# Meta keys' share of the attention outputs: one stacked fp32r product in place of one float32 product

## The chip, the cores and the metric

The kernel runs on one core of one Trainium2 chip. The metric is the device time of one execution in microseconds (us), the median of several runs. TensorE (PE) does the matrix products, with loads of the stationary operand (PEld) as records of their own; VectorE is DVE, ScalarE is ACT, GpSimd is POOL, and SyncE (SP) issues the DMAs.

## The reference, cut to what matters

Two layers; each has an input projection of 9,216 columns, eight HGRN2 heads, eight differential-attention heads and an output projection. There are 512 tokens and 16 meta tokens in front of them, 528 rows in all. The part that the change touches is this:

```
s = einsum('bqhcd,bkhcd->bhcqk', qblk, kh) * scale     # 528 keys, the first 16 are the meta tokens
p = softmax(s, axis=-1)
p_diff = p[:, :, 0] - lam * p[:, :, 1]
o      = einsum('bhqk,bkhv->bqhv', p_diff, vh)          # 528 keys contracted: 4 x 128 + 16
```

## The kernel before

Everything is kept transposed, features in partitions and tokens in columns. A projection unit is a tile of 128 output columns, accumulated over 8 pieces; each piece is three fp32r products (high weight by high input, high by low, low by high), in two halves of 264 tokens or, where the meta rows are not wanted, once over 512 (`piece`, L1797). The heads of a layer come one after another; each is cut into steps, and after each step `feed` puts some pieces of the next head's units, of the output projection's too, into TensorE's program. All orders are written out by hand, in five programs (SP, POOL, ACT, DVE, PE) that meet in semaphores.

An attention head (heads 8 to 15 of a layer) works in chunks of 128 queries, two steps to a chunk, one for each of the two softmax components. Layer 0 has five chunks (the fifth is the 16 meta queries), layer 1 has four. For chunk i and component comp, step s = 2i + comp does, engine by engine:

- PE: waits for the exponential of step s-1 (`exp_done`), then computes the scores into `pair` (L2041, L2043). In odd steps from 3 on it turns the difference of the softmaxes of chunk j = i-1: four 128-column transposes (L2072) and one of the 16 meta columns (L2073), into `main` and `meta`. In even steps from 4 on it computes the output of chunk j = i-2 (L2058, L2060), then come the fed pieces.
- DVE: the row maximum (`neg_max`, L1652) of each step; in even steps from 2 on, L1671, L1673 and L1681 make the difference `qk_dec` of chunk j = i-1 and raise `p_ready`. Between them stand the halves' cut of the weights (`w_lo`, L1265), the scaled copies out of PSUM (L1330), the rotary turn (L1424, L1426, L1437, L1442) of the next head's queries and keys, and the low parts of the stacked queries and keys (L1449).
- ACT: the exponential of each step (L1078, with a second record for its sum); `copy_turned`, which brings the turned probabilities to SBUF (L1061 the four blocks, L1064 the meta block; raises `pt_ready`); the output rows (L1091, L1098); the high cut of the weights (`w_hi`, L848); and `stack_high`, the high parts of the next head's stacked queries and keys (L1112), which for the keys waits for DVE's L1442.

ACT's program of a layer-1 head has the keys' `stack_high` in step 8 and `copy_turned` of chunk 3 in step 9, so the second stands behind the first.

The output of one chunk:

```
for kk in range(4):
    pe.matmul(meta[:, 0:P], cols[:, kk, :], v_main(kk), start=(kk == 0), stop=False)
pe.matmul(meta[:, 0:P], cols[:, 4, :], v_meta[:, :], start=False, stop=True).then_inc(pv_done, 1)
```

All five are float32. The last contracts 128 rows, of which 16 are meta keys and the rest zero. `v_meta` is made by `turn_v` (a transpose of 16 columns, L1898) and ACT's `copy_v`.

Of the kernel before, what the change touches and what calls it, by code (L numbers as in the profile page):

```python
# [31 lines left out]
P = 128  # L32
DEPTH = 2
D_MODEL = 1024
N_META = 16
# [3 lines left out]
HG_HEADS = 8  # L39
AT_HEADS = 8  # L40
# [14 lines left out]
LEVELS = 8  # L55
META_LEVELS = 5
HG_TILES = ("zf", "zb", "q", "v", "g")
AT_TILES = ("aq", "ak", "av", "ag")
# [296 lines left out]
def encoder_trunk(nc, x_t, w_units, norm_g, lb_logits, hg_gain, lambdas, at_gain, final_g,  # L355
# [9 lines left out]
    with ctx:  # L365
# [56 lines left out]
        lam_in = state_f[:, :, :].rearrange("p a (b d) -> p a b d", b=2)  # L422
        lam_prod = state_b[:, 0:DEPTH, :].rearrange("p a (b d) -> p (a b) d", b=2)
        score = sb("score", [P, N_CHUNKS, P])
        blend = sb("blend", [P, N_CHUNKS, HALF_CHUNK])
# [49 lines left out]
        v_written = sem("v_written")  # L475
        v_landed = sem("v_landed")
        v_turned = sem("v_turned")
        v_ready = sem("v_ready")
# [214 lines left out]
        def facing_totals(m, first):  # L693
# [7 lines left out]
                           ap=[at.ap[0], [stride, 2], [2, n_pairs], [0, m]])  # L701

        def v_main(j):

            return v_rows[:, :, j, :]
# [89 lines left out]
        def _(pool):  # L795
# [8 lines left out]
            pool.memset(k_low[:, :, :].bitcast(f32), 0.0).then_inc(pads_set, 1)  # L804
            pool.memset(parity[:, :, :], 0.0).then_inc(pads_set, 1)

            def invert_rms(n):

                pool.wait_ge(sq_ready, n + 1)
                if n > 0:  # L810
                    pool.wait_ge(o_scaled, n)
                pool.tensor_scalar(o_inv[:, :], o_sums[:, :], P * NORM_EPS, None, ALU.add)\
                    .then_inc(pool_step, 1)
                pool.wait_ge(pool_step, n + 1)
                pool.tensor_tensor(o_inv[:, :], o_inv[:, :], minus_half[:, :], ALU.pow)\
                    .then_inc(o_inv_ready, 1)

            def cut_mixed(n):
# [6 lines left out]
            for l in range(DEPTH):  # L825
                for c in range(HEADS):
                    n = l * HEADS + c
                    if c > 0:
                        cut_mixed(n - 1)
                    invert_rms(n)  # L830
                cut_mixed(l * HEADS + HEADS - 1)
# [3 lines left out]
        def _(act):  # L835
# [121 lines left out]
            def copy_v(n):  # L957
                act.wait_ge(v_turned, n + 1)
                act.activation(v_meta[0:N_META, :], meta[0:N_META, 0:P], ACT.Copy).then_inc(v_ready, 1)

# [96 lines left out]
            def copy_turned(a, j, chunks_before):  # L1057
# [5 lines left out]
                                    ACT.Copy))  # L1063
                act.activation(cols[0:N_META, 4, 0:rows], meta[0:N_META, 0:rows], ACT.Copy)\  # L1064
                    .then_inc(pt_ready, 1)

# [57 lines left out]
            act.wait_ge(ones_set, 4)  # L1124
            act.wait_ge(pads_set, 6)
            load_root_table()
# [73 lines left out]
        def _(dve):  # L1200
# [455 lines left out]
            def attend(l, c, s):  # L1656
# [10 lines left out]
                if comp == 0 and 1 <= i < 1 + chunks:  # L1667
# [8 lines left out]
                    if j >= 2:  # L1676
# [4 lines left out]
                    dve.scalar_tensor_tensor(qk_dec[r, j % 2, 0, :], e1, row_inv[r, j % 2, 1:2], e0,  # L1681
                                             ALU.mult, ALU.add).then_inc(p_ready, 1)

            dve.wait_ge(gain_in, 16)
# [85 lines left out]
        def _(pe):  # L1770
# [120 lines left out]
            def turn_v(l, c):  # L1891
# [4 lines left out]
                if l * HEADS + c > 0:  # L1896
                    pe.wait_ge(o_taken, l * HEADS + c)
                pe.transpose(meta[0:N_META, 0:P], v_t[:, 0:N_META], ident[:, :]).then_inc(v_turned, 1)  # L1898

# [125 lines left out]
            def attend(l, c, s):  # L2025
# [26 lines left out]
                if comp == 0 and 2 <= i < 2 + chunks:  # L2052
# [4 lines left out]
                    for kk in range(4):  # L2057
                        pe.matmul(meta[:, 0:P], cols[:, kk, :], v_main(kk),  # L2058
                                  start=(kk == 0), stop=False)
                    pe.matmul(meta[:, 0:P], cols[:, 4, :], v_meta[:, :],  # L2060
                              start=False, stop=True).then_inc(pv_done, 1)
                if comp == 1 and 1 <= i < 1 + chunks:
# [8 lines left out]
                    for kk in range(4):  # L2071
                        pe.transpose(main[:, kk * P:kk * P + rows], p[:, chunk(kk)], ident[0:rows, 0:rows])  # L2072
                    pe.transpose(meta[0:N_META, 0:rows], p[:, 0:N_META], ident[0:rows, 0:rows])\  # L2073
                        .then_inc(p_turned, 1)
# [119 lines left out]
```

## Time and profile before

| | |
|---|---|
| runs of the kernel before | 1397.12 us median of 3 (1396.78 to 1397.17) |
| the profiled execution | 1397.53 us, its span 1395.7 us |
| granted clock of TensorE, mean | 0.999 of full speed |
| busy | PE 1381.9 us, DVE 1045.8, ACT 801.0, POOL 101.0 |
| attention heads | layer 0 from about 356 to 700 us, layer 1 from about 1050 to 1358 us |
| a middle attention head | 37.5 us in layer 0, 34.3 us in layer 1 |

A matrix product's record lasts longer than its share of the engine, since the next one starts under it; the distance from start to start is what a product costs in a dense stretch. In the timeline a row with x8 is eight records in a run, from the first one's start to the last one's end.

### The profile page before, as it was taken

To read this page: it belongs to the slowest core of one execution; us is meant where nothing else is said; L and a number is where in the kernel's file an instruction comes from. 1 tells how busy PE (TensorE), PEld (TensorE's weight loads), DVE (VectorE), ACT (ScalarE), POOL (GpSimd) and SP (SyncE) were. 2 spreads that over 40 slices of the span, in tenths; PEclk is the share of its full clock that TensorE was granted. 3 is DMA by queue.
4 is the path that set the end of the run, shared out by engine and by line. 5 is a ranking of instruction groups with operands and counts; after the bars stand their busy time and mean duration, and the time that the engine had idled before them with its cause. 6 is when DMAs were issued, how large, how long until landed. Compare 5 with 4: busy or idle time off the path is not lost.

```text
span 1395.7 us, 32289 instructions
## 1 busy us (share of the span) xinstructions
PE 1381.9 (99%) x13212; PEld 1302.6 (93%) x13212; DVE 1045.8 (75%) x1819; ACT 801.0 (57%) x1738; POOL 101.0 (7%) x110
## 2 busy tenths in 40 slices
PE   9999999999999999999999999999999999999998
PEld 9999999999999999999998888988888899999987
DVE  6888778788646777877667788888886477777764
ACT  7666666655434655566555666666663355555554
POOL 0001000000000000000000011111100000000000
PEclk9999999999999999999999999999999999999999
DMA  5322222232323233322233222233223323333322
GB/s 187 107 91 77 92 83 73 91 92 62 100 75 100 84 85 92 92 78 83 69 107 106 92 77 85 83 93 92 92 78 98 91 86 95 95 95 94 94 91 76
DMA packets 57619, 126.77 MB, mean 91 GB/s; under 512 B 7424, under 2 KB 24064, under 8 KB 57472
## 3 DMA queue, kind: packets, MB, share of 16 engines
q1 hardware_dynamic: 57472, 124.71, 29.3%
q8 instruction: 105, 1.72, 0.5%
q14 instruction: 42, 0.34, 0.1%
HBM read 105.54 MB, written 10.49 MB: 83 GB/s over the span
## 4 chain that ended last, share of the span: by engine, by line
PE 92%; DVE 3%; ACT 2%; issue 2%; DMA 1%; SPq 0%; DVEq 0%; ACTq 0%
PE proj L1797 66%; PE far L2058 5%; PE pair L2041 3%; PE pair L2043 3%; PE far L2072 2%; PE pair L1930 2%; PE far L2060 1%; PE far L2011 1%; PE far L2012 1%; PE pair L1992 1%; PE far L1947 1%; PE pair L1797 1%; PE pair L1999 1%; PE far L2015 1%; PE far L1930 1%
## 5 line engine op out<-in xcount | busy, mean ns | idle before, releaser
L1797 PE MATMUL proj<-u_hi,w_hi 128*128 128x264 f32 (+1 forms) x1960 | 479.5, 313 | 2.2 <-DVE w_lo L1265 0.8
L1797 PE MATMUL proj<-u_hi,w_lo 128*128 128x264 f32 (+1 forms) x1960 | 458.0, 302 | 0.0
L1797 PE MATMUL proj<-u_lo,w_hi 128*128 128x264 f32 (+1 forms) x1960 | 457.9, 302 | 0.0
L1797 PEld LDWEIGHTS proj<-u_hi,w_hi 128*128 128x128 f32 x1960 | 314.5, 189 | 19.7 <-issue 1.5
L1797 PEld LDWEIGHTS proj<-u_hi,w_lo 128*128 128x128 f32 x1960 | 313.8, 188 | 13.5
L1797 PEld LDWEIGHTS proj<-u_lo,w_hi 128*128 128x128 f32 x1960 | 314.0, 188 | 10.6
L1265 DVE TENSOR_TENSOR w_lo<-w_raw,w_hi 128x1024 fp32r<-128x1024 f32 x178 | 220.8, 1241 | 39.6 <-ACT w_hi L848 39.5
L1078 ACT ACTIVATE decay<-pair,neg_max 128x528 f32<-128x528 f32 (+1 forms) x144 | 100.4, 697 | 219.1 <-DVE neg_max L1652 218.9
L848 ACT ACTIVATE w_hi<-w_raw 128x1024 fp32r<-128x1024 f32 x178 | 186.7, 1049 | 43.6 <-PE proj L1797 40.4
L1652 DVE TENSOR_REDUCE neg_max<-pair 128x1 f32<-128x528 f32 (+1 forms) x144 | 101.4, 704 | 98.1 <-PE pair L2043 97.9
L1797 PE MATMUL proj<-mix_hi,w_hi 128*128 128x264 f32 (+1 forms) x364 | 99.5, 329 | 0.0
L1538 DVE TENSOR_TENSOR ops<-ops,totals 128x528 f32<-128x528 f32 (+1 forms) x96 | 66.7, 695 | 41.7 <-ACT decay L1000 23.6
L1797 PE MATMUL proj<-mix_lo,w_hi 128*128 128x264 f32 (+1 forms) x364 | 96.3, 320 | 0.0
L1797 PE MATMUL proj<-mix_hi,w_lo 128*128 128x264 f32 (+1 forms) x364 | 96.2, 320 | 0.0
L821 POOL TENSOR_TENSOR mix_lo<-mixed_t,mix_hi 128x528 fp32r<-128x528 f32 (+1 forms) x32 | 42.5, 1329 | 617.4 <-ACT mix_hi L1122 617.4
L2058 PE MATMUL far<-v_rows,cols 128*128 128x128 f32 x576 | 77.4, 277 | 0.2
L2041 PE MATMUL pair<-k_stack,q_stack 128*128 128x264 f32 x288 | 76.8, 287 | 0.0
L2043 PE MATMUL pair<-k_low,q_stack 128*128 128x264 f32 x288 | 76.2, 285 | 0.0
L2058 PEld LDWEIGHTS far<-v_rows,cols 128*128 128x128 f32 x576 | 70.5, 191 | 4.0 <-ACT cols L1064 2.8
L1547 DVE TENSOR_TENSOR ops<-ops,totals 128x528 f32<-128x528 f32 (+1 forms) x96 | 66.3, 690 | 0.0
L1797 PEld LDWEIGHTS proj<-mix_hi,w_lo 128*128 128x128 f32 x364 | 60.2, 188 | 5.0
L1797 PEld LDWEIGHTS proj<-mix_hi,w_hi 128*128 128x128 f32 x364 | 60.2, 189 | 4.9
(254 smaller groups left out, 2167.8 us busy)
## 6 DMA issues: line engine op xcount, KB each, us to landing
w_raw<-w_units SPq DMA_DIRECT2D x178, 512.0 KB, 3.5
v_scratch<-v_blocks SPq DMA_DIRECT2D x128, 64.0 KB, 2.5
v_rows<-v_scratch SPq DMA_DIRECT2D x32, 256.0 KB, 2.9
q_stack<-gate_f SPq DMA_DIRECT2D x32, 132.0 KB, 2.4
k_stack<-k_stack SPq DMA_DIRECT2D x32, 132.0 KB, 2.3
h<-x_t SPq DMA_DIRECT2D x8, 264.0 KB, 5.6
cos_sin<-rope SPq DMA_DIRECT2D x2, 528.0 KB, 5.9
out_t<-ops SPq DMA_DIRECT2D x2, 512.0 KB, 3.5
```

The source lines that it names most:

```text
L821: pool.tensor_tensor(mix_lo[:, n % 8, ts], mixed_t[:, ts], mix_hi[:, n % 8, ts].bitcast(f32), ALU.subtract)\
L848: act.activation(w_hi[:, u % N_CUT, :, :], w_raw[:, u % N_RAW, :, :], ACT.Copy)\
L1078: act.activation(two(decay[0:rows, 2 * (i % 2) + comp, :]), pair[0:rows, :, both], ACT.Exp, bias=neg_max[0:rows, i % 2, comp:comp + 1], ac ...
L1265: dve.tensor_tensor(w_lo[:, u % N_CUT, :, :], w_raw[:, u % N_RAW, :, :], w_hi[:, u % N_CUT, :, :].bitcast(f32), ALU.subtract).then_inc(lo_ ...
L1538: dve.tensor_tensor(keys, keys, facing_totals(m, KF), ALU.mult).then_inc(k_widened, 1)
L1547: dve.tensor_tensor(queries, queries, facing_totals(m, QB), ALU.mult).then_inc(qk_ready, 1)
L1652: dve.tensor_reduce(neg_max[0:rows, i % 2, comp:comp + 1], pair[0:rows, :, both], axis=mybir.AxisListType.XY, op=ALU.max, negate=True)\
L1797: ins = pe.matmul(out, w, x[:, tile, cols_n], start=(k == 0 and p == 0), stop=(k == last_k and p == 2))
L1930: ins = pe.matmul(level_result(lv)[b * BLOCK:(b + 1) * BLOCK, j, to:to + wide], keys[:, at:at + BLOCK], queries[:, facing:facing + wide], ...
L2041: pe.matmul(pair[0:rows, b, both], q_stack[:, comp, cs], k_stack[:, comp, keys], start=True, stop=False)
L2043: ins = pe.matmul(pair[0:rows, b, both], q_stack[:, comp, cs], k_low[:, comp, keys], start=False, stop=True)
L2058: pe.matmul(meta[:, 0:P], cols[:, kk, :], v_main(kk), start=(kk == 0), stop=False)
```

## The change

The 16 meta columns of the probabilities and the 16 meta rows of the values are each cut into a high part rounded to fp32r and the rest as a low part. The parts are laid side by side, values as high, high, low, low and probabilities as high, low, high, low, so that after the turn 64 rows are contracted and one fp32r product holds all four cross products. New instructions: two on DVE for each chunk, two on POOL for each attention head. The transposes of the meta columns take 64 columns in place of 16, ACT's two meta copies have 64 partitions in place of 16, and PE waits for the new parts ahead of the meta transposes.

```diff
+        v_parts = sb("v_parts", [P, PARTS], f32r)          # PARTS = 4 * N_META = 64
+        v_stack = sb("v_stack", [P, P], f32r)
+        p_parts = sb("p_parts", [P, 2, PARTS], f32r)
+        p_stack = sb("p_stack", [P, P], f32r)
...
+        def twice(x):
+            return x.unsqueeze(1).to_broadcast([x.shape[0], 2, N_META])
+        def value_parts(low):
+            return v_parts[:, 2 * low * N_META:2 * (low + 1) * N_META].rearrange("p (a n) -> p a n", a=2)
+        def prob_parts(rows, j, low):
+            return p_parts[rows, j % 2, :].rearrange("p (a b n) -> p a b n", a=2, b=2)[:, :, low, :]
...
 # POOL
+            pool.memset(v_stack[:, :].bitcast(f32), 0.0).then_inc(pads_set, 1)
+            pool.memset(p_stack[:, :].bitcast(f32), 0.0).then_inc(pads_set, 1)
+            def split_values(l, c):
+                a = l * AT_HEADS + c - HG_HEADS
+                t = l * LAYER_UNITS + value_unit(c)
+                pool.wait_ge(evacuated[t % 2], evac_count(t))
+                now = v_t[:, 0:N_META]
+                pool.tensor_scalar(value_parts(0), twice(now), 1.0, None, ALU.mult).then_inc(v_split, 1)
+                pool.wait_ge(v_split, 2 * a + 1)
+                pool.tensor_tensor(value_parts(1), twice(now), value_parts(0).bitcast(f32), ALU.subtract)\
+                    .then_inc(v_split, 1)
...
                     if c > 0:
                         cut_mixed(n - 1)
+                    if HG_HEADS <= c + 1 < HEADS:
+                        split_values(l, c + 1)
                     invert_rms(n)
 # ACT
-                act.activation(v_meta[0:N_META, :], meta[0:N_META, 0:P], ACT.Copy).then_inc(v_ready, 1)
+                if n % HEADS < HG_HEADS:
+                    act.activation(v_meta[0:N_META, :], meta[0:N_META, 0:P], ACT.Copy).then_inc(v_ready, 1)
+                else:
+                    act.activation(v_stack[0:PARTS, :], meta[0:PARTS, 0:P], ACT.Copy).then_inc(v_ready, 1)
...
-                act.activation(cols[0:N_META, 4, 0:rows], meta[0:N_META, 0:rows], ACT.Copy)\
-                    .then_inc(pt_ready, 1)
+                act.activation(p_stack[0:PARTS, 0:rows], meta[0:PARTS, 0:rows], ACT.Copy).then_inc(pt_ready, 1)
 # DVE, behind L1681
+                    dve.wait_ge(p_ready, chunks_before + j + 1)
+                    now = twice(qk_dec[r, j % 2, 0, 0:N_META])
+                    dve.tensor_copy(prob_parts(r, j, 0), now).then_inc(p_split, 1)
+                    dve.wait_ge(p_split, 2 * (chunks_before + j) + 1)
+                    dve.tensor_tensor(prob_parts(r, j, 1), now, prob_parts(r, j, 0).bitcast(f32), ALU.subtract)\
+                        .then_inc(p_split, 1)
 # PE
-                pe.transpose(meta[0:N_META, 0:P], v_t[:, 0:N_META], ident[:, :]).then_inc(v_turned, 1)
+                if c < HG_HEADS:
+                    pe.transpose(meta[0:N_META, 0:P], v_t[:, 0:N_META], ident[:, :]).then_inc(v_turned, 1)
+                else:
+                    pe.wait_ge(v_split, 2 * (l * AT_HEADS + c - HG_HEADS + 1))
+                    pe.transpose(meta[0:PARTS, 0:P], v_parts[:, :].bitcast(f32), ident[:, :]).then_inc(v_turned, 1)
...
-                    pe.matmul(meta[:, 0:P], cols[:, 4, :], v_meta[:, :],
+                    pe.matmul(meta[:, 0:P], p_stack[:, :], v_stack[:, :],
                               start=False, stop=True).then_inc(pv_done, 1)
...
-                    pe.transpose(meta[0:N_META, 0:rows], p[:, 0:N_META], ident[0:rows, 0:rows])\
+                    pe.wait_ge(p_split, 2 * (chunks_before + j + 1))
+                    pe.transpose(meta[0:PARTS, 0:rows], p_parts[0:rows, j % 2, :].bitcast(f32), ident[0:rows, 0:rows])\
                         .then_inc(p_turned, 1)
```

## Rows read from the trace of the kernel before

**Rows 1.** The page, part 1: busy us, share of the span, instructions.
```profile
PE 1381.9 (99%) x13212; PEld 1302.6 (93%) x13212; DVE 1045.8 (75%) x1819; ACT 801.0 (57%) x1738; POOL 101.0 (7%) x110
```

**Rows 2.** The page, part 4: chain that ended last, shares by engine.
```profile
PE 92%; DVE 3%; ACT 2%; issue 2%; DMA 1%; SPq 0%; DVEq 0%; ACTq 0%
```

**Rows 3.** Windows, one layer-1 head: stretch, length, busy PE, PEld, DVE, ACT, POOL, clock, DMA.
```profile
1159.30:1193.70 34.40, 34.39 (x245) 31.80 (x242) 26.85 (x44) 20.05 (x50) 2.72 (x3) 1.00 0.33 93
```

**Rows 4.** Waits of the whole span: us in total, times, longest us.
```profile
ACT k_stack L1112 <- DVE gate_f L1442: 7.3, 6, 1.2
...
PEld far L2058 <- ACT cols L1064: 2.8, 6, 0.5
```

**Rows 5.** Groups by line and shape, TensorE: busy us, mean ns, idle before.
```profile
L2060 PE MATMUL far<-v_meta,cols 128*128 128x128 f32 x144 | 27.8, 275 | 0.0
```

**Rows 6.** Timeline of PE, layer-1 head, output of chunk 2: start, us, instruction.
```profile
1179.71 1.05 PE L2058 MATMUL far<-v_rows,cols 128*128 128x128 f32 x8
1180.60 0.39 PE L2060 MATMUL far<-v_meta,cols 128*128 128x128 f32 x2
...
1181.07 0.41 PE L1797 MATMUL proj<-u_lo,w_hi 128*128 128x264 f32 x2
1181.32 0.41 PE L1797 MATMUL proj<-u_hi,w_lo 128*128 128x264 f32 x2
```

**Rows 7.** Groups by line and shape, VectorE: small instructions.
```profile
L1671 DVE RECIPROCAL row_inv<-row_sum 128x2 f32<-128x2 f32 x64 | 9.8, 153 | 0.2 <-ACT decay L1078 0.2
...
L1496 DVE TENSOR_TENSOR totals<-totals 128x32 f32<-128x32 f32 x16 | 3.0, 186 | 0.0
```

**Rows 8.** Timeline of DVE, the same layer-1 head, steps 6 to 9.
```profile
1175.62 0.77 DVE L1681 SCALAR_TENSOR_TENSOR qk_dec<-decay,row_inv 128x528 f32<-128x528 f32 x1
1177.16 0.71 DVE L1652 TENSOR_REDUCE neg_max<-pair 128x1 f32<-128x528 f32 x1 [0.77 <-PE pair L2043]
...
1177.80 0.76 DVE L1424 STREAM_SHUFFLE stage<-stage 128x528 f32<-128x528 f32 x1
1178.59 0.71 DVE L1426 TENSOR_TENSOR stage<-stage,cos_sin 128x528 f32<-128x528 f32 x1
...
1180.87 0.77 DVE L1681 SCALAR_TENSOR_TENSOR qk_dec<-decay,row_inv 128x528 f32<-128x528 f32 x1
1181.55 0.70 DVE L1437 TENSOR_TENSOR stage<-stage,cos_sin 128x528 f32<-128x528 f32 x1
1182.29 0.71 DVE L1442 TENSOR_TENSOR gate_f<-stage 128x528 f32<-128x528 f32 x1
```

**Rows 9.** Timeline of ACT, the same steps.
```profile
1175.88 0.19 ACT L1078 ACTIVATION_READ_ACCUMULATOR decay<-pair,neg_max 128x1 f32 x1
...
1183.03 1.31 ACT L1112 ACTIVATE k_stack<-gate_f 64x528 fp32r<-64x528 f32 x2 [1.20 <-DVE gate_f L1442]
...
1184.87 0.25 ACT L1064 ACTIVATE cols<-far 16x128 f32<-16x128 f32 x1
```

**Rows 10.** Timeline of TensorE's loads, the same steps.
```profile
1176.35 0.19 PEld L2041 LDWEIGHTS pair<-k_stack,q_stack 128*128 128x128 f32 x1
...
1176.85 0.47 PEld L2072 LDWEIGHTS far<-ident,qk_dec 128*128 128x128 f32 x4
1177.29 0.09 PEld L2073 LDWEIGHTS far<-ident,qk_dec 128*16 128x16 f32 x1
...
1185.17 0.41 PEld L2058 LDWEIGHTS far<-v_rows,cols 128*128 128x128 f32 x3 [0.45 <-ACT cols L1064]
```

**Rows 11.** Timelines of ACT and of the loads, a layer-0 head, step 7.
```profile
603.60 0.19 ACT L1078 ACTIVATION_READ_ACCUMULATOR decay<-pair,neg_max 128x1 f32 x1
...
603.99 0.19 PEld L2041 LDWEIGHTS pair<-k_stack,q_stack 128*128 128x128 f32 x1
```

**Rows 12.** Timeline of DVE, layer 1's last head, behind the difference of chunk 1.
```profile
1341.21 0.77 DVE L1681 SCALAR_TENSOR_TENSOR qk_dec<-decay,row_inv 128x528 f32<-128x528 f32 x1
1342.11 1.38 DVE L1386 TENSOR_TENSOR h<-h,proj 128x512 f32<-128x512 f32 x2
```

More of the change, by code:

```diff
@@ L56 @@
 META_LEVELS = 5
+PARTS = 4 * N_META
 HG_TILES = ("zf", "zb", "q", "v", "g")
@@ L476, in encoder_trunk @@
         v_landed = sem("v_landed")
+        v_split = sem("v_split")
+        p_split = sem("p_split")
         v_turned = sem("v_turned")
@@ L1124, in _ @@
             act.wait_ge(ones_set, 4)
-            act.wait_ge(pads_set, 6)
+            act.wait_ge(pads_set, 8)
             load_root_table()
```

## The prediction, made before the changed kernel was run

> **What bounds the kernel now.** First the page: TensorE is busy for 99% of the span [rows 1] and carries 92% of the chain that ended last [rows 2]. So what TensorE is spared comes off the time one for one, unless TensorE then waits. Next, the windows view says where spare time lies on the other engines: in one middle head of layer 1, 34.40 us long, PE is busy for 34.39, DVE for 26.85, ACT for 20.05 and POOL for 2.72 [rows 3]. DVE is 78% full, with its program in a fixed order, so its idle time need not lie where the new instructions are. Last, the waits: ACT's high cut of the stacked keys waits for DVE's L1442 six times, 7.3 us in all, and PE's output products wait for ACT's meta copy six times [rows 4]. Six is the number of middle heads of layer 1, so in each of them there is a place where TensorE already stands still behind ACT, which stood behind DVE. The reader is to keep this place in mind: a delay of DVE ahead of it costs TensorE the same delay.
>
> **What the change takes from TensorE.** The meta product leaves 144 records, two for each of the 72 products (8 heads by 5 chunks and 8 by 4) [rows 5]. Eight float32 records start within 0.89 us, 0.111 us apart [rows 6]; a product costs two, 0.222 us. The new one is one record. No fp32r product of 128 columns is in this trace. Two fp32r records of 264 columns take 0.25 us from start to start [rows 6], so by columns alone 128 would cost 0.061. From above I know no row dearer than what it replaces, 0.222. Between them lies one float32 record, 0.111, which streams 128 columns and loads 128: the new record has the same load. I take that: the next product's load needs its time whatever the stream takes. The gain is 72 x 0.111 = 8.0 us at most, 11.6 by columns alone, 0 at the price of float32.
>
> A page of the Trainium skill speaks against the 0.061: "TensorE: Matmul & The Clock Gate", section "LDWEIGHTS (loading the stationary operand)", has a load's time as its columns over 1.2, in ns. For 128 columns that is 107 ns, an estimate, close to the 111 of the row; the gain would be 72 x 0.115 = 8.3 us instead of the 11.6. No run here shows a load by itself yet.
>
> **What it leaves alone.** The transposes of meta columns keep 128 streamed columns. Their load grows from 16 to 64 columns, but four transposes whose loads have 128 columns follow at (1177.29 - 1176.85)/4 = 0.11 us [rows 10], so 64 hide as well. ACT's meta copies have as many elements to a partition as before (0.25 us [rows 9]), only more partitions: nothing. POOL gets two short instructions for each of 16 heads; it is busy 2.72 us of a head of 34.40 [rows 3], and the values are wanted only in step 1 of the next head. What stands behind them in POOL's queue, the output's root mean square, is wanted there too. I price both at nothing; if POOL were late, DVE's scaling in step 1 would be. The two extra memsets are at the start, ahead of ACT's first wait, some tenths at most.
>
> **What it adds on DVE.** Behind each L1681 a copy and a subtraction of 32 elements, each waiting for the one before. A dependent instruction of DVE starts 0.79 us after one of 0.76 (L1424, L1426), so 0.03 after its end; an independent one starts 0.68 us after an L1681 of 0.77, so 0.09 ahead of its end [rows 8]. Small instructions take 0.153 and, at 32 elements, 0.186 [rows 7]. From the start of L1681: copy at 0.80, subtraction at 0.80 + 0.19 + 0.03 = 1.02 at most, and with 0.18 for the copy 1.01; its end at 1.20; the next instruction at 1.11. It was 0.68. So DVE's stream is put back by **0.43 us for each chunk**, 31 us in all. From below, two copies at 0.15 that overlap give 0.30; from above, 0.65, if each hand-over costs 0.14 more, as the 0.90 us from L1681 to its follower in the last head [rows 12] would suggest.
>
> **Where that lands, a middle head of layer 1 (six of them).** The cut of chunk 1 is followed by a dense stretch that ends with chunk 2's L1681; the row maximum of step 6 and its exponential are inside it. That exponential's last record ends at 1175.88 + 0.19 = 1176.07 [rows 9], and the first load of step 7's scores, which waits for it, started at 1176.35 [rows 10]. With 0.06 us for the hand-over the slack is 0.22. Late by 0.43, it makes PE late by 0.21, and the 0.22 us that PE saved in the outputs of chunks 0 and 1 are gone too, since they only let it come earlier to the same wait. The cut of chunk 2 puts DVE 0.86 us back in all; the idle 0.77 ahead of step 7's row maximum [rows 8] takes that down to 0.09, less than PE's own 0.21. So the maximum starts 0.21 late. From it to L1442 DVE has no gap [rows 8], and chunk 3's cut lies within: L1442 is 0.21 + 0.43 = 0.64 late, and so are ACT's L1112, which had waited 1.20 us for it, the copies behind it to 1185.12 [rows 9], and PE's loads, which started 0.05 later at 1185.17 after waiting [rows 10]. Chunk 3's own saving still comes off. A head gets 0.64 - 0.11 = 0.53 us longer, six 3.2 us. The wait for the parts themselves costs nothing: chunk 2's subtraction ends at 1175.62 + 0.43 + 1.20 = 1177.25, and the meta load was at 1177.29 [rows 8, 10], 0.21 later now.
>
> **A middle head of layer 0 (six).** The same wait in step 7: 603.79 to 603.99 [rows 11], slack 0.14 with the hand-over. PE is 0.29 late. Behind it no key cut waits for DVE (all six waits of [rows 4] are layer 1's), so the savings of chunks 2 to 4 stay: 0.29 - 0.33 = -0.04, six -0.2 us.
>
> **The other four heads.** The first of each layer is long, with slack of microseconds: both keep their saving, 9 x 0.111 = 1.0 us. In the last ones L1386 follows L1681 after 0.90 us [rows 12], now after 1.11: 0.21 late, and its followers with it; then chunks 1 to 4 and 1 to 3 save 0.44 and 0.33. Together 0.42 - 0.77 = -0.35 us.
>
> **Sum.** 3.2 - 0.2 - 1.0 - 0.35 = **+1.6 us**. The profiled execution took 1397.53 us, with a span of 1395.7; it is 0.4 us above the median of 1397.12, so the span would be 1397.3 and the median **1398.7**. What a measurement of this kernel can tell from no change is about 0.2%, 2.8 us: the same. Each 0.1 us more or less on DVE for a chunk is worth 6 x 2 + 6 + 2 = 20 times that, 2 us.
>
> **The rivals.**
> 1. The gain comes through: the slacks are taken up by idle time that I don't see, or the pacing settles differently with a faster PE. 1397.1 - 8.0 = 1389.1. For it: 99% and 92% [rows 1, 2], and half of DVE's idle time is in pieces like the 0.77 of [rows 8]. Against it: the six waits of [rows 4], where the slack is nil.
> 2. The change does not do what it says: an fp32r product of 128 columns costs what the float32 one did. Then the savings go and the delays stay: 6 x 0.64 + 6 x 0.29 + 2 x 0.21 = +6.0, 1403.1. For it: nothing in the trace shows a short fp32r product at a good rate. Against it: its long products run at one column for about 0.47 ns [rows 6], with a load each. [...]
> 3. DVE's hand-overs are dear, the mechanism of the forecast with another price: at 0.65 us for a chunk, 1.6 + 20 x 0.22 = +6.0, 1403.1. It decides for slower from 0.43 + 1.2/20 = 0.49 us on. For it: [rows 12]. Against it: the 0.03 of [rows 8].
>
> **How the numbers follow.** Forecast 0.38, rival 1 0.22, rival 2 0.22, rival 3 0.18. The likeliest alone, with 0.30 to 0.49 us on DVE, is 1396.1 to 1399.9. Faster by over 0.2% (below 1394.3): rival 1 and little besides, 0.24. Slower (above 1399.9): rivals 2 and 3 but for their mild halves, 0.36. The same: 0.40. The range has to reach both sides, 1389 to 1404.
>
> **What would show it.** In the profile after: L2060 with 72 records and the next product starting 0.11 us after the meta record's share (0.22 if rival 2 holds); the stretch from L1681 to the next DVE instruction at 1.11 us in dense places; ACT's wait for L1442 above 7.3 us and PE's wait for L1064 grown by 0.5 us for each of six heads; middle heads of layer 1 near 34.9 us, of layer 0 near 37.5. The prediction is wrong if the layer-1 heads got shorter: then the chain through L1112 was not as tight as its idle times say. It is wrong too if PE waits at the meta transposes.

## The result, and the profile of the changed kernel

| | before | after |
|---|---|---|
| median, us (lowest to highest, runs) | 1396.9 (1396.45 to 1397.67, 18) | 1399.74 (1399.08 to 1401.56, 18) |
| span of the profiled execution, us | 1395.7 | 1397.9 |
| mean granted clock of TensorE | 0.999 | 0.999 |

The change costs 2.84 us: the ratio is 1.0021, with a 95% interval of 1.0013 to 1.0028. I had forecast +1.6 us and "the same" within 0.2%. The sign is right and the size 1.2 us short. The ratio lies just beyond 0.2%; the median lies 0.16 us under the 1399.9 at which the prediction began "slower", so a little more of the same delays would have made it that.

A comparison of lines needs their new numbers: the piece is L1839, the scores L2087 and L2089, the output products L2104, the meta product L2106, the transposes L2118 and L2120, ACT's copies L1098 and L1101, its keys L1148; DVE's difference L1717 with the new copy L1721 and subtraction L1723, its row maximum L1688, the rotary turn's last two L1473 and L1478.

First the page of after, parts 1 and 4:

```profile
PE 1379.5 (99%) x13140; PEld 1297.1 (93%) x13140; DVE 1071.4 (77%) x1963; ACT 802.1 (57%) x1738; POOL 111.5 (8%) x144
...
PE 84%; DVE 8%; issue 4%; ACT 3%; DMA 0%; SPq 0%; POOL 0%; DVEq 0%; ACTq 0%; POOLq 0%
```

PE has 72 records less than in [rows 1] and is busy for 2.4 us less, yet the span is 2.2 us longer: outside its records PE now stands for 18.4 us instead of 13.8. DVE has 144 instructions more, 25.6 us. In the chain PE's share went from 92% to 84% and DVE's from 3% to 8% [rows 2].

The groups by line and shape of after (busy us, mean ns of one, idle before):

```profile
L2106 PE MATMUL far<-v_stack,p_stack 128*128 128x128 f32 x72 | 22.1, 307 | 0.0
...
L2120 PEld LDWEIGHTS far<-ident,p_parts 128*64 128x64 f32 x64 | 7.1, 111 | 0.0
...
L1721 DVE CAST p_parts<-qk_dec 128x32 fp32r<-128x32 f32 x64 | 13.6, 212 | 2.2
...
L1723 DVE TENSOR_TENSOR p_parts<-qk_dec,p_parts 128x32 fp32r<-128x32 f32 x64 | 12.3, 192 | 2.2
```

The meta product is one record now. Its mean of 307 ns beside the 275 of [rows 5] is no price; the distance of the starts is. The timeline of PE in after, at the place of [rows 6] (PE = TensorE):

```profile
1179.93 1.05 PE L2104 MATMUL far<-v_rows,cols 128*128 128x128 f32 x8
1180.73 0.31 PE L2106 MATMUL far<-v_stack,p_stack 128*128 128x128 f32 x1
1180.88 0.47 PE L1839 MATMUL proj<-u_hi,w_hi 128*128 128x264 f32 x2
1181.18 0.42 PE L1839 MATMUL proj<-u_lo,w_hi 128*128 128x264 f32 x2
```

From the start of the last of the eight float32 records to that of the third record of the pieces behind (1181.18 here) it is 0.476 us in this head, where it was 0.581. Over the 57 of 72 outputs that have the same dense stretch behind them the medians are 0.470 and 0.581: the product takes 0.111 us less, as forecast.

The windows view of the head of [rows 3] in after (its own length, which starts at the same 1159.30):

```profile
1159.30:1194.25 34.95, 34.35 (x241) 31.56 (x239) 28.34 (x52) 20.13 (x50) 3.29 (x5) 1.00 0.31 92
```

It is 0.55 us longer, with PE busy for 34.35 us where it was 34.39. Where PE stands still is read from the waits of after (us in total, times, longest us):

```profile
ACT k_stack L1148 <- DVE gate_f L1478: 10.1, 6, 1.7
...
PEld far L2104 <- ACT p_stack L1101: 6.3, 7, 1.0
...
PEld pair L2087 <- ACT decay L1114: 3.7, 13, 0.3
```

The first was 7.3 us and the second 2.8 [rows 4]; the third, the scores behind the exponential of the step before, was 0.2 us, once. The timelines of the same head, DVE's first:

```profile
1176.09 0.77 DVE L1717 SCALAR_TENSOR_TENSOR qk_dec<-decay,row_inv 128x528 f32<-128x528 f32 x1
1176.89 0.18 DVE L1721 CAST p_parts<-qk_dec 128x32 fp32r<-128x32 f32 x1
1177.11 0.19 DVE L1723 TENSOR_TENSOR p_parts<-qk_dec,p_parts 128x32 fp32r<-128x32 f32 x1
1177.39 0.71 DVE L1688 TENSOR_REDUCE neg_max<-pair 128x1 f32<-128x528 f32 x1
...
1181.10 0.77 DVE L1717 SCALAR_TENSOR_TENSOR qk_dec<-decay,row_inv 128x528 f32<-128x528 f32 x1
1181.90 0.18 DVE L1721 CAST p_parts<-qk_dec 128x32 fp32r<-128x32 f32 x1
1182.12 0.19 DVE L1723 TENSOR_TENSOR p_parts<-qk_dec,p_parts 128x32 fp32r<-128x32 f32 x1
1182.22 0.70 DVE L1473 TENSOR_TENSOR stage<-stage,cos_sin 128x528 f32<-128x528 f32 x1
1182.96 0.71 DVE L1478 TENSOR_TENSOR gate_f<-stage 128x528 f32<-128x528 f32 x1
```

ACT's (after):

```profile
1176.35 0.19 ACT L1114 ACTIVATION_READ_ACCUMULATOR decay<-pair,neg_max 128x1 f32 x1
...
1183.70 1.32 ACT L1148 ACTIVATE k_stack<-gate_f 64x528 fp32r<-64x528 f32 x2 [1.67 <-DVE gate_f L1478]
1185.04 0.60 ACT L1098 ACTIVATE cols<-far 128x512 f32<-128x512 f32 x1
1185.54 0.26 ACT L1101 ACTIVATE p_stack<-far 64x128 fp32r<-64x128 f32 x1
```

And the loads' (after):

```profile
1176.60 0.19 PEld L2087 LDWEIGHTS pair<-k_stack,q_stack 128*128 128x128 f32 x1 [0.25 <-ACT decay L1114]
...
1177.52 0.11 PEld L2120 LDWEIGHTS far<-ident,p_parts 128*64 128x64 f32 x1
...
1185.85 0.74 PEld L2104 LDWEIGHTS far<-v_rows,cols 128*128 128x128 f32 x6 [1.00 <-ACT p_stack L1101]
```

Behind L1717 the next instruction starts after 1.12 us (1182.22 - 1181.10), where it was 0.68 [rows 8]: 0.44 for a chunk. The scores of step 7 start at 1176.60 instead of 1176.35, the keys' high parts at 1183.70 instead of 1183.03 [rows 9], the last outputs at 1185.85 instead of 1185.17 [rows 10]. That last shift of 0.68, less chunk 3's own saving of 0.11, gives 0.57; the head is 0.55 longer. The load of the meta transposes starts at 1177.52, 0.22 after the end of the subtraction, with no wait.

### The profile page after: what moved, and what is told of

The parts are those of the page before. It is cut to its first block, busy times and chain, and to the rows that moved or that the text cites. A ratio compares the mean times of both kernels' runs of the same rounds, so it can differ in the third digit from the quotient of the medians.

```text
span 1397.9 us, 32323 instructions
## 1 busy us (share of the span) xinstructions
PE 1379.5 (99%) x13140; PEld 1297.1 (93%) x13140; DVE 1071.4 (77%) x1963; ACT 802.1 (57%) x1738; POOL 111.5 (8%) x144
## 4 chain that ended last, share of the span: by engine, by line
PE 84%; DVE 8%; issue 4%; ACT 3%; DMA 0%; SPq 0%; POOL 0%; DVEq 0%; ACTq 0%; POOLq 0%
PE proj L1839 61%; PE far L2104 3%; PE pair L2087 3%; PE pair L2089 2%; PE far L2118 2%; PE pair L1976 2%; PE far L2057 1%; PE far L2058 1%; DVE w_lo L1301 1%; PE pair L2038 1%; DVE stage L1460 1%; DVE neg_max L1688 1%; PE far L1993 1%; PE pair L1839 1%; DVE qk_dec L1717 1%
## 5 line engine op out<-in xcount | busy, mean ns | idle before, releaser
L1839 PE MATMUL proj<-u_hi,w_hi 128*128 128x264 f32 (+1 forms) x1960 | 477.6, 312 | 2.9 <-ACT stage L961 1.2
L1839 PE MATMUL proj<-u_hi,w_lo 128*128 128x264 f32 (+1 forms) x1960 | 458.2, 302 | 0.0
L1839 PE MATMUL proj<-u_lo,w_hi 128*128 128x264 f32 (+1 forms) x1960 | 457.9, 302 | 0.0
L1839 PEld LDWEIGHTS proj<-u_hi,w_hi 128*128 128x128 f32 x1960 | 314.7, 189 | 19.1 <-issue 2.2
L1839 PEld LDWEIGHTS proj<-u_hi,w_lo 128*128 128x128 f32 x1960 | 314.0, 188 | 13.5
L1839 PEld LDWEIGHTS proj<-u_lo,w_hi 128*128 128x128 f32 x1960 | 314.0, 188 | 10.6
L1688 DVE TENSOR_REDUCE neg_max<-pair 128x1 f32<-128x528 f32 (+1 forms) x144 | 101.3, 704 | 82.5 <-PE pair L2089 79.6
L1839 PE MATMUL proj<-mix_hi,w_hi 128*128 128x264 f32 (+1 forms) x364 | 99.1, 327 | 0.1
L1839 PE MATMUL proj<-mix_lo,w_hi 128*128 128x264 f32 (+1 forms) x364 | 96.2, 320 | 0.0
L1839 PE MATMUL proj<-mix_hi,w_lo 128*128 128x264 f32 (+1 forms) x364 | 96.1, 320 | 0.0
L2104 PE MATMUL far<-v_rows,cols 128*128 128x128 f32 x576 | 77.7, 278 | 3.4 <-ACT p_stack L1101 3.4
L2087 PE MATMUL pair<-k_stack,q_stack 128*128 128x264 f32 x288 | 79.2, 295 | 0.8
L2104 PEld LDWEIGHTS far<-v_rows,cols 128*128 128x128 f32 x576 | 70.4, 191 | 7.1 <-ACT p_stack L1101 6.3
L2089 PE MATMUL pair<-k_low,q_stack 128*128 128x264 f32 x288 | 76.1, 285 | 0.0
L1839 PEld LDWEIGHTS proj<-mix_hi,w_lo 128*128 128x128 f32 x364 | 60.3, 188 | 5.0
L1839 PEld LDWEIGHTS proj<-mix_hi,w_hi 128*128 128x128 f32 x364 | 60.2, 189 | 4.8 <-POOL mix_lo L853 0.4
```

The source lines that it names most:

```text
L1688: dve.tensor_reduce(neg_max[0:rows, i % 2, comp:comp + 1], pair[0:rows, :, both], axis=mybir.AxisListType.XY, op=ALU.max, negate=True)\
L1839: ins = pe.matmul(out, w, x[:, tile, cols_n], start=(k == 0 and p == 0), stop=(k == last_k and p == 2))
L2087: pe.matmul(pair[0:rows, b, both], q_stack[:, comp, cs], k_stack[:, comp, keys], start=True, stop=False)
L2089: ins = pe.matmul(pair[0:rows, b, both], q_stack[:, comp, cs], k_low[:, comp, keys], start=False, stop=True)
```

## The experiments

Every kernel was timed in five rounds beside the kernel before, on the same chip as it; "from before" is the difference to the median of before in those rounds (1396.87 to 1397.32). The 95% interval of such a ratio is about 0.0009 to 0.0013 to either side, 1.3 to 1.8 us, so smaller differences of medians rest on the heads of the profiles. The "heads" are distances between the transposes of v that open each head (L1944 in after), in the profiled execution: H0 is layer 0's first attention head, M0 its six middle ones together, H1 and M1 the same in layer 1, each as its difference from before. One profile carries some noise besides: the stretch ahead of the first of these heads was 0.1 to 1.1 us shorter than in the profile of before in every kernel, whatever it changed, and in six of the profiles one head of layer 0 is 0.4 to 1.5 us longer than its neighbours. In the table these are the second head with the product alone (+0.23 where the other five have -0.51 to -0.53) and with POOL's cuts and the late turn (+0.55, the others -0.24 to -0.26). In all six PE's loads wait at the end of that head for the keys' DMA, 0.36 to 1.7 us.

| kernel | median, us | from before | H0 | M0 | H1 | M1 |
|---|---|---|---|---|---|---|
| after | 1399.74 | +2.8 | -0.21 | +0.31 | -0.15 | +3.28 |
| product alone | 1391.00 | -6.0 | -0.55 | -2.36 | -0.43 | -1.44 |
| DVE's cuts alone | 1403.27 | +6.3 | +0.31 | +1.65 | +0.30 | +3.76 |
| third copy on DVE | 1406.82 | +9.8 | -0.02 | +3.49 | +0.03 | +6.00 |
| cuts on POOL | 1402.19 | +5.3 | -1.11 | +2.94 | -0.97 | +3.73 |
| cuts on POOL, late turn | 1395.24 | -2.1 | -0.83 | -0.71 | -0.96 | -1.27 |

**The product without the cuts.** From before; the two tiles are fp32r with 16 rows filled, and the low parts are left out, so that the meta keys' share carries the rounding of fp32r.

```
-                act.activation(cols[0:N_META, 4, 0:rows], meta[0:N_META, 0:rows], ACT.Copy)\
+                act.activation(p_stack[0:N_META, 0:rows], meta[0:N_META, 0:rows], ACT.Copy)\
...
-                    pe.matmul(meta[:, 0:P], cols[:, 4, :], v_meta[:, :],
+                    pe.matmul(meta[:, 0:P], p_stack[:, :], v_stack[:, :],
```

> The kernel before with the meta product alone as one fp32r product of 16 rounded rows; no cuts, no low parts (the meta share is left rounded). Theory of the prediction: the new product costs one record of 0.11 us where two stood. No instruction of DVE is added, so all 40 savings of layer 0 stay (4.4 us); in layer 1 a middle head keeps three of four, since the output of chunk 3 waits for a chain that starts in step 7, and the last and first keep theirs: 0.44 + 6 x 0.33 + 0.33 = 2.8 us. Sum -7.2 us, some 0.5% faster. Rival, the short fp32r product costs what the float32 one did: within 0.5 us of the kernel before. Rival, savings in the first heads are lost (they gave back only 0.2 us there in the changed kernel): -6.5 us.

Measured 1391.00 us (1390.71 to 1391.81), ratio 0.9958 [0.9945, 0.997]: 6.0 us of the 8.0 that 72 products save, and 1.2 short of the -7.2 expected. The first heads keep all of theirs (9 x 0.111 = 1.0, measured 0.98), the middle heads of layer 1 only 0.24 each of 0.44, where 0.33 was expected; 0.75 us is the one long head of layer 0. The keys' wait of [rows 4] reads, in this kernel's waits:

```profile
ACT k_stack L1117 <- DVE gate_f L1447: 8.2, 6, 1.4
```

With a faster PE, ACT comes to this place earlier and waits longer for DVE (7.3 us before), and PE's output products behind it wait 3.5 us in all instead of 2.8.

**DVE's cuts without the product.** From before; nobody reads `p_parts`.

```
                                              ALU.mult, ALU.add).then_inc(p_ready, 1)
+                    dve.wait_ge(p_ready, chunks_before + j + 1)
+                    now = twice(qk_dec[r, j % 2, 0, 0:N_META])
+                    dve.tensor_copy(prob_parts(r, j, 0), now).then_inc(p_split, 1)
+                    dve.wait_ge(p_split, 2 * (chunks_before + j) + 1)
+                    dve.tensor_tensor(prob_parts(r, j, 1), now, prob_parts(r, j, 0).bitcast(f32), ALU.subtract)\
+                        .then_inc(p_split, 1)
```

> The kernel before with DVE's two cut instructions behind each difference, and nobody who reads or awaits them; product, transposes, POOL and ACT as before. Theory: the whole loss is DVE's stream, put back 0.44 us for each chunk. Middle heads of layer 1 longer by about 0.65 us (4.0 us for six), of layer 0 by 0.3 (1.8 us), the last heads 0.4 together: +6.2 us, 0.44% slower. Rival, the loss in layer 1 comes from PE's new wait, the 64-column transposes or POOL's cuts: within 1 us of the kernel before.

Measured 1403.27 us (1403.08 to 1403.81), 1.0045 [1.0032, 1.0058], +6.3. M1 is 0.63 for each head where 0.64 was worked out, M0 0.27 for 0.29. So the two small instructions alone carry the whole loss, as expected. With the product alone at -6.0, a plain sum would be +0.3, but both together give +2.8: some 2.5 us of the product's saving exist only as long as DVE is not late, since they lie ahead of a wait for DVE.

**The whole change with a float32 product.** From after:

```
-        v_stack = sb("v_stack", [P, P], f32r)
+        v_stack = sb("v_stack", [P, P])
...
-        p_stack = sb("p_stack", [P, P], f32r)
+        p_stack = sb("p_stack", [P, P])
```

> The changed kernel with the stacked product left in float32: all added work and waits stay, only the saving on TensorE goes. Theory: as with DVE's cuts alone, +6.2 us against the kernel before, that is 3.4 us above the changed kernel; two records for each meta product again. If waits for the parts, POOL or the transposes cost anything of their own, it is above the run with DVE's cuts alone by that much. Rival, the fp32r product saves nothing: the same as the changed kernel, +2.8 us.

Measured 1403.58 us (1403.4 to 1403.88), 1.0047 [1.0033, 1.006], +6.6. The product is two records again, and its distance 0.581 as before:

```profile
L2106 PE MATMUL far<-v_stack,p_stack 128*128 128x128 f32 x144 | 27.8, 275 | 0.0
```

So the fp32r form is worth 3.8 us inside the whole change, and all that the whole change has beside DVE's two instructions and the product (POOL's cuts of the values, the wider transposes, PE's waits for the parts) costs 6.6 - 6.3 = 0.3 us, less than the medians of two such rounds can tell from nothing.

**A third small copy on DVE.** From after, 0.22 us more for a chunk:

```
+                    dve.wait_ge(p_split, 2 * (chunks_before + j + 1))
+                    step(dve.tensor_copy(spare[r, :, :], now))
```

> The changed kernel with a third dependent DVE instruction of 32 elements behind the two cuts, whose result nobody reads. Theory: each 0.1 us on DVE for a chunk is worth 20 x 0.1 = 2 us; 0.21 us more make +4.3 us over the changed kernel, +7.1 over the kernel before, most of it in six heads of layer 1 (0.42 each) and six of layer 0 (0.2 to 0.4 each). Rival, DVE has idle time enough and something else costs the time: within 1 us of the changed kernel.

The timeline of DVE in this kernel shows the stretch from L1718 to its follower at 1.34 us:

```profile
1185.68 0.77 DVE L1718 SCALAR_TENSOR_TENSOR qk_dec<-decay,row_inv 128x528 f32<-128x528 f32 x1
1186.48 0.18 DVE L1722 CAST p_parts<-qk_dec 128x32 fp32r<-128x32 f32 x1
1186.70 0.19 DVE L1724 TENSOR_TENSOR p_parts<-qk_dec,p_parts 128x32 fp32r<-128x32 f32 x1
1186.92 0.18 DVE L1727 COPY spare<-qk_dec 128x32 f32<-128x32 f32 x1
1187.02 0.70 DVE L1474 TENSOR_TENSOR stage<-stage,cos_sin 128x528 f32<-128x528 f32 x1
```

Measured 1406.82 us (1406.57 to 1407.69), 1.0072 [1.0059, 1.0084]: 7.1 us over after, where 4.3 was expected. Beside the fp32r product the first 0.44 us on DVE cost 8.8 us (from the product alone, -6.0, to after, +2.8), 20 us for each us, which is the prediction's own price; without the product they cost 6.3, 14 for each. The next 0.22 cost 7.1, 32 for each. Layer 1 follows the working: 0.45 a head, expected 0.42. Layer 0 doesn't: 0.53 a head, expected 0.2 to 0.4. The waits show where, first in after, then in this kernel:

```profile
PEld pair L2087 <- DMA k_stack<-k_stack: 0.4, 2, 0.2
...
PEld pair L2090 <- DMA k_stack<-k_stack: 2.1, 6, 0.4
```

These are the first scores of the next head behind the DMA of its keys, in each of the six middle heads of layer 0. Up to step 9 the third copy makes such a head 0.21 us later than in after, and the rest of the 0.53 comes at this wait. A slope read off one wait per head holds only until the slack at the next wait is used up.

**The keys' cuts one step later.** In layer 1 ACT's keys then stand behind `copy_turned` of chunk 3. Made from before and from after:

```
-    return (TURN_KEYS, TURN_KEYS + 1) if c < HG_HEADS else (last, last + 1)
+    return (TURN_KEYS, TURN_KEYS + 1) if c < HG_HEADS else (last, last + (2 if l == LAST else 1))
...
-    return (TURN_KEYS + 1, TURN_KEYS + 2) if c < HG_HEADS else (last + 1, last + 1)
+    return (TURN_KEYS + 1, TURN_KEYS + 2) if c < HG_HEADS else (last + 1, last + (2 if l == LAST else 1))
```

> The kernel before with one move: in layer 1 ACT's high cut of the next head's stacked keys, and DVE's low cut of them, stand one step later, behind ACT's copy of chunk 3's turned probabilities. Theory: that copy no longer waits for DVE's rotary turn, and the 0.2 to 0.3 us that TensorE stands still there goes in six heads: -1.2 to -1.8 us. Rival, the keys are then late for the next head's first scores, which wait for their stacking: slower by 1 us or more.

> The changed kernel with the same move. Theory: the 0.43 us that each of six layer-1 heads lost at the output of chunk 3, and the 0.2 to 0.3 us that it waited there in the kernel before, go: 0.6 to 0.7 us a head, about 3.9 us below the changed kernel, 1395.8, so 1 us faster than the kernel before. The loss at the scores of step 7 stays. Rival, the chunk 3 wait is not the keys' order but DVE's whole load: less than 1 us below the changed kernel.

Measured 1395.08 us from before (1394.74 to 1395.32, 11 runs), 0.9987 [0.9978, 0.9996], -1.8; and 1394.94 from after (1394.58 to 1396.27, 11 runs), 0.9986 [0.9977, 0.9995], which is -1.9 from before and -4.8 from after. The timeline of ACT in the first of them:

```profile
1182.20 0.60 ACT L1061 ACTIVATE cols<-far 128x512 f32<-128x512 f32 x1 [1.21 <-PE far L2073]
1182.70 0.24 ACT L1064 ACTIVATE cols<-far 16x128 f32<-16x128 f32 x1
1182.86 1.30 ACT L1112 ACTIVATE k_stack<-gate_f 64x528 fp32r<-64x528 f32 x2
```

The keys' wait for DVE is gone, and PE's loads of the last outputs start at 1183.91 without one. M1 is -1.85 from before and -1.72 from after. So the chain through the keys' cut is what makes layer 1's heads longer: in the moved order the change costs nothing that the rounds can tell (1394.94 beside 1395.08, in the same rounds). It gains nothing either. The 24 cheaper products of these heads, 2.7 us, still don't come through, and step 7's scores come late behind the exponential as in after (3.7 us in 13 waits in both). The second profile has a head of layer 0 that is 1.39 us longer, where PE waits for the keys' DMA; the move is in layer 1 alone, so I take it for one of the single long heads.

**The cuts on POOL.** The same two instructions for the probabilities, from DVE to the engine with 2.72 of 34.40 us busy [rows 3]; from after, and once more with the keys later. DVE's two instructions go, and in POOL's program the cut of chunk 0 stands ahead of `cut_mixed` (`mix_lo`), that of the other chunks behind it:

```
+            def split_probs(l, c, j):
...
+                pool.tensor_scalar(prob_parts(r, j, 0), now, 1.0, None, ALU.mult).then_inc(p_split, 1)
+                pool.wait_ge(p_split, 2 * at + 1)
+                pool.tensor_tensor(prob_parts(r, j, 1), now, prob_parts(r, j, 0).bitcast(f32), ALU.subtract)\
+                    .then_inc(p_split, 1)
```

> The changed kernel with the two cuts of each chunk's meta probabilities on POOL in place of DVE. Theory: DVE's stream is again that of the kernel before, so the savings of TensorE come through as with the product alone (-6.0 us), less what PE waits for POOL's parts: two instructions of 0.31 us and two hand-overs, ready some 0.7 to 0.8 us after the difference where DVE's were after 0.43, and the transposes wanted them after 0.67 to 0.9: 0 to 0.1 us for each chunk of the middle heads, 0 to 3 us in all. 1391 to 1394. Rival, POOL's instructions hold up DVE's for as long as they run, as its cut of the mixed outputs seems to: then DVE is put back as before and the time is 1397 or more.

> The cuts on POOL and the keys' cut later together. Theory: the two act at different places, so 1 to 2 us below the run with the cuts on POOL: 1389 to 1392. Rival, once DVE is free of the cuts the order is worth nothing more: the same as with the cuts on POOL.

Both missed; 1391 to 1394 and 1389 to 1392 were expected. Measured 1402.19 us (1401.37 to 1402.51), 1.0037 [1.0024, 1.005], and 1402.03 (1401.73 to 1402.64), 1.0037 [1.0025, 1.005]: +5.3 and +5.2. The waits of the first show a new place:

```profile
PEld far L2131 <- POOL p_parts L859: 15.3, 27, 0.8
...
PE far L2131 <- POOL p_parts L859: 8.3, 18, 0.5
```

PE waits at the meta transposes. The timelines of DVE, POOL and the loads there (same kernel):

```profile
1170.85 1.22 DVE L1318 TENSOR_TENSOR w_lo<-w_raw,w_hi 128x1024 fp32r<-128x1024 f32 x1
...
1171.02 1.19 POOL L857 TENSOR_SCALAR p_parts<-qk_dec 128x32 fp32r<-128x32 f32 x1 [0.91 <-DVE qk_dec L1734]
...
1172.29 0.25 POOL L859 TENSOR_TENSOR p_parts<-qk_dec,p_parts 128x32 fp32r<-128x32 f32 x1
...
1172.60 0.11 PEld L2131 LDWEIGHTS far<-ident,p_parts 128*64 128x64 f32 x1 [0.73 <-POOL p_parts L859]
```

POOL's first instruction takes 1.19 us and ends 0.14 us behind DVE's w_lo; where DVE is between instructions it takes 0.29 or 0.30. The reverse, the rival, doesn't hold: beside POOL's short cuts DVE's instructions keep their times (w_lo 1.22 us with or without one, the rotary turn's 0.70 and 0.71). From the start of the difference to the end of the subtraction it is 1.21 us with DVE (1177.30 - 1176.09 in after), and with POOL 1.48, 2.38, 1.48 and 2.24 for the four chunks of this head. The slack at the transposes was 0.22 in after. With PE held there, the order of the keys is worth nothing (1402.03 beside 1402.19).

The first heads gain more than with the product alone, -1.11 and -0.97 instead of -0.55 and -0.43. `mix_lo` now runs behind DVE's gates, which take 0.70 us there instead of the 1.84 of before, and PE's wait for ACT behind them (0.35 and 0.26 us in before) is gone. That part of the gain is an order on POOL and not the product.

**PE's meta transposes later.** Behind the first piece fed in the step, with the wait for the parts; the four big transposes stay. From after, from the kernel with POOL's cuts, and from the latter with the keys later too:

```
+                for at, (u, k) in enumerate(fed_pieces(c)[pieces_by(c, s - 1):pieces_by(c, s)]):
+                    piece(l, u, k)
+                    if at == 0 and turns:
+                        turn_meta_probs(l, c, i - 1)
+                        turns = False
...
-                    pe.wait_ge(p_split, 2 * (chunks_before + j + 1))
-                    pe.transpose(meta[0:PARTS, 0:rows], p_parts[0:rows, j % 2, :].bitcast(f32), ident[0:rows, 0:rows])\
-                        .then_inc(p_turned, 1)
```

> The changed kernel (cuts on DVE) with PE's transposes of the meta parts, and their wait, behind the first fed piece of the step, 0.7 us later. Theory: PE's wait for the parts costs nothing where DVE cuts, so nothing changes: within 0.7 us of the changed kernel, 1399.7. Rival, a part of the loss is that wait: 1 us or more below it.

> Cuts on POOL, and PE's transposes of the meta parts behind the first fed piece. Theory from the cuts on POOL: TensorE stood still 27 times and 15 us on its loads for parts that POOL finished late, since POOL's instruction stretches from 0.30 to 1.2 us while DVE runs one with two inputs; with 0.7 us more to the deadline most of that is hidden, and the time is near the product alone: 1391 to 1393. Rival, POOL's instructions hold up DVE as much as DVE holds POOL: above 1395.

> The same with the keys' cut of layer 1 one step later. Theory: the keys' order alone gave 1.8 us, and its place is another than PE's wait for the parts: 1.5 to 2 us below the run before it, 1389 to 1391.5. Rival: with a free DVE the order is worth nothing.

From after it measured 1405.83 us (1404.52 to 1407.71), 1.006 [1.0047, 1.0073]: +8.5 from the 1397.32 of before in those rounds, 5.7 us more than after's +2.8, where no change was expected. Layer 1 is as in after (M1 +3.23), so there the wait for the parts had cost nothing; M0 went to +4.11, 0.40 to 0.57 in five heads and 1.91 in one. The last heads and what follows them are 1.9 us longer than in after. The waits of this kernel have PE's scores behind the keys' DMA, and the outputs behind ACT's copy, more than after has (0.4 us in 2 and 6.3 in 7):

```profile
PEld pair L2102 <- DMA k_stack<-k_stack: 2.9, 6, 1.7
...
PEld far L2119 <- ACT p_stack L1101: 8.4, 11, 1.0
```

By the trace, a middle head of layer 0 runs as in after up to step 9, and the whole loss stands at the next head's first scores, which wait for the keys' DMA in all six (0.18 to 0.36 us, and 1.70 in the long one). The four more waits for ACT's copy are in the two last heads, 0.32 to 0.58 us each. `copy_turned` waits for the meta block and comes later, and with it what stands behind it. In the fourth middle head, against after and counted from the head's start, chunk 3's copy is 0.73 us later, the exponential behind it 0.55, DVE's difference of chunk 4 and the low cut of the queries 0.54 and 0.55, and the second keys' DMA 0.55. That is the order of the trace; no run tried one link alone.

With POOL's cuts the same move helps: 1395.24 us (1394.21 to 1397.19, 11 runs), 0.9985 [0.9976, 0.9994], -2.1 from before (of 1397.32 in those rounds), where the same kernel without it had +5.3. With the keys later as well it is **1393.44 us** (1392.37 to 1395.21, 9 runs), 0.9974 [0.9964, 0.9984], -3.9: the fastest that computes everything, M1 -3.68. Both were expected lower, at 1391 to 1393 and 1389 to 1391.5. The first lies 3.1 us of span over the product alone (1392.6 and 1389.5). The late turn brings waits that the product alone doesn't have: the outputs of the last heads stand behind ACT's meta copy four times (0.32 and 0.47 us in layer 0, 0.58 and 0.57 in layer 1), and these heads with what follows them are 1.9 us longer than there; layer 0's middle heads are 1.6 us longer. Nor is all of the -3.9 the product's: the keys' order gives 1.8 us without the change, and the first heads' order on POOL about 0.8.

## Why the prediction was right, and where it was off

**The product.** One record, 0.111 us less: as forecast. Rival 2 is wrong; the float32 form in the same place costs 3.8 us more. The Trainium skill ("TensorE: Matmul & The Clock Gate", "LDWEIGHTS (loading the stationary operand)") has a load at its columns over 1.2 in ns; 107 for 128 columns, an estimate from it, is near the 0.111 of the trace. Whether it is the load or the stream that sets the distance no run tells apart.

**DVE.** 0.44 us for a chunk instead of 0.43, with hand-overs of 0.03. Rival 3, which wanted 0.49 or more, had the wrong price.

**The middle heads of layer 1.** +3.28 us instead of +3.2. The places are the forecast ones: step 7's scores 0.25 late (0.21 forecast), ACT's keys, L1112 before and L1148 now, 0.67 (0.64), the last outputs 0.68. The wait of ACT for L1478 grew by 2.8 us and PE's for ACT's copy by 3.5 (0.3 of it one more of them, in layer 0), against 6 x 0.5 = 3 forecast. DVE's cuts alone give the delay without the savings, and the keys later take the loss away. Rival 1, the gain coming through, fails here; it is real in what the product does alone, -6.0 us.

**The middle heads of layer 0.** +0.31 instead of -0.2, a term mis-sized by 0.5 us. Step 7's scores come 0.28 to 0.31 us late against the head's start (0.29 forecast), and by step 9 the shift is 0.14 to 0.18, with one saving of 0.11 taken off: as forecast so far. Then I had looked at one wait in the head. "Behind it no key cut waits for DVE" leaves out the keys' DMAs. SyncE issues them (L740) behind the DMAs of the queries (L736), and these wait for DVE's low cut of the queries (L1485): 84.3 us in 15 waits of SyncE in after. The cuts of chunks 3 and 4 stand ahead of that low cut in DVE's program. In the fourth of the middle heads it ends 0.79 us later than in before, counted from the head's start, and the second of the keys' DMAs is issued 0.74 us later. In four of the six heads PE's loads then stand idle for the keys at the next head's first scores, 0.18, 0.12, 0.07 and 0.20 us; these heads are 0.07 to 0.21 longer than before, the two without such a wait 0.07 and 0.10 shorter. The four waits are 0.57 us together, the size of the miss.

**The first heads.** -0.36 instead of -1.0: the step that failed, "with slack of microseconds". The savings of 0.98 are there in the product alone, and the cuts alone lose 0.61. The waits that I had not read are in step 2 of the first head. Timeline of before, DVE, ACT and PE:

```profile
366.18 1.84 DVE L1420 SCALAR_TENSOR_TENSOR gates<-stage 128x528 f32<-128x528 f32 x1
...
368.11 0.61 ACT L927 ACTIVATE stage<-proj 128x528 f32<-128x528 f32 x1 [2.30 <-DVE gates L1420]
...
368.87 0.48 PE L1797 MATMUL proj<-u_hi,w_hi 128*128 128x264 f32 x2 [0.35 <-ACT stage L927]
```

and of after:

```profile
365.73 1.20 DVE L1721 CAST p_parts<-qk_dec 128x32 fp32r<-128x32 f32 x1
366.96 0.19 DVE L1723 TENSOR_TENSOR p_parts<-qk_dec,p_parts 128x32 fp32r<-128x32 f32 x1
367.07 0.70 DVE L1456 SCALAR_TENSOR_TENSOR gates<-stage 128x528 f32<-128x528 f32 x1
...
367.87 0.61 ACT L961 ACTIVATE stage<-proj 128x528 f32<-128x528 f32 x1 [2.62 <-DVE gates L1456]
...
368.62 0.48 PE L1839 MATMUL proj<-u_hi,w_hi 128*128 128x264 f32 x2 [0.67 <-ACT stage L961]
```

The pieces there want the PSUM tile that ACT frees behind DVE's gates. PE waited 0.35 us already, with no slack, and now waits 0.67; in the first head of layer 1 it is 0.57 instead of 0.26. The two together, 0.63 us, are the missing part.

**The sum.** The forecast was a span of 1397.3. First heads +0.6, layer 0's middle heads +0.5 and layer 1's +0.1 more than said; the last heads and the rest -0.1; together +1.1. With the 1.6 that is 2.7, and the medians have 2.84. The spans differ by only 2.2, since the stretch ahead of the first attention head is 0.57 us shorter in this profile than in that of before; the profiled execution of before took 1397.53, 0.6 above the median of its 18 runs.

**PE and the parts.** "PE waits at the meta transposes" did not happen with the cuts on DVE (load at 1177.52 after a subtraction that ends at 1177.30), and did with them on POOL.

## What to carry to other kernels

When work leaves the engine that is busy for 99% and small work lands on one that is busy for 75%, follow the second engine's program from each addition to the next wait of the first one, in every kind of stage: a few such waits without slack in each head took back more than 72 cheaper products gave. The product and the cuts were worth -6.0 and +6.3 us alone and +2.8 together, so parts of a change are not to be added where they meet in a wait. Before small work is put on an idle engine, look at how long its instructions take beside a busy neighbour. Before giving a change up, try the order of what stands behind the late result (here 4.8 us for one step's shift), and try the same order without the change: 1.8 of the 4.8 are there too, and the change in the moved order is worth nothing.

## What the hardware showed that I had not expected

- GpSimd and VectorE can hold each other up. POOL's first cut, 32 elements, takes 0.29 or 0.30 us alone, and 0.68 or 1.19 beside DVE instructions with two inputs in SBUF; beside those with one of two inputs in PSUM (`h`, from `proj`) it stays at 0.29. DVE's 32-element cast takes 0.18 us, and 1.20 and 1.16 in the two places where it falls into POOL's two-input `mix_lo` (1.57 and 1.52 us); in before, L1420 takes 1.84 and 1.78 there instead of 0.70. POOL's short cuts hold no instruction of DVE measurably. The Trainium skill, "GPSIMD Engine Reference", "Specifications", says that POOL's SBUF interfaces are shared with VectorE, with contention for DVE instructions that have two SBUF inputs. The trace agrees. The held cast has one input; what of the two engines' access it shares with `mix_lo` no trace here tells.
- An fp32r product with 128 streamed columns takes 0.11 us of a dense stretch, half of a float32 one (0.222 us less the 0.111 saved).
